# Cached memory in seven buffers with its heads side by side, and a convolution spread over more stages, in a one-core decoder trunk

## The reference

```python
def conv_branch(glu, prev, dw_w, dw_b, ln_g, ln_b):
    xp = jnp.concatenate([prev, glu], axis=1)
    y = lax.conv_general_dilated(xp, dw_w[:, None, :], window_strides=(1,), padding='VALID',
                                 dimension_numbers=('NWC', 'WIO', 'NWC'),
                                 feature_group_count=CONV_WIDTH)
    y = layer_norm(y + dw_b, ln_g, ln_b)
    return jax.nn.silu(y), xp[:, -(CONV_K - 1):]

def cross_attention(xn, mem_k, mem_v, w_xq, w_xo):
    B, T, _ = xn.shape
    q = (xn @ w_xq).reshape(B, T, N_X_HEADS, X_HEAD_DIM)
    s = jnp.einsum('bqhd,bkhd->bhqk', q, mem_k).astype(jnp.float32) * X_SCALE
    p = jax.nn.softmax(s, axis=-1).astype(mem_v.dtype)
    o = jnp.einsum('bhqk,bkhd->bqhd', p, mem_v).reshape(B, T, D_MODEL)
    return o @ w_xo
```

## Time and profile before

| what | value |
|---|---|
| median of 3 runs (lowest to highest) | 2113.44 us (2112.59 to 2114.67) |
| the profiled execution: time, span | 2116.94 us, 2115.4 us |
| mean granted TensorE clock | 0.941 |
| busy: PE, PEld, DVE, ACT, POOL | 89%, 81%, 46%, 24%, 6% of the span |
| chain that ended last, by engine | PE 81%, DVE 8%, ACT 4%, issue 3%, DMA 3% |
| moved by DMA | 187.11 MB, mean 88 GB/s |

### The profile page before, as it was taken

One profiled execution on the slowest core, in us unless ns is written; L12 is line 12 of the kernel. 1 busy time (PEld: TensorE's weight loads), 2 busy tenths in 40 slices (PEclk: granted clock), 3 DMA queues, 4 the chain that ended last, 5 costly groups with the idle time before them and its releaser, 6 DMA issues.

```text
span 2115.4 us, 33154 instructions
## 1 busy us (share of the span) xinstructions
PE 1872.2 (89%) x13009; PEld 1705.1 (81%) x13009; DVE 969.3 (46%) x1131; ACT 500.1 (24%) x762; POOL 137.0 (6%) x200
## 2 busy tenths in 40 slices
PE   6699997887777897899896996999999999999993
PEld 5699895666554796799763995999999999999992
DVE  2625677887445528532320329343223343233445
ACT  3421114665334211310431224111000100001122
POOL 0000002211121002000001002000000000000001
PEclk7899998999899898899997998999999999999995
DMA  6311116655484312401125022121111111111004
GB/s 159 123 40 60 59 60 190 213 169 161 151 284 164 122 40 66 153 20 63 36 76 203 20 55 87 40 59 40 40 52 47 40 42 58 40 40 55 30 15 164
DMA packets 133052, 187.11 MB, mean 88 GB/s; under 512 B 7912, under 2 KB 99242, under 8 KB 132454
## 3 DMA queue, kind: packets, MB, share of 16 engines
q1 hardware_dynamic: 112816, 103.96, 15.8%
q0 software_dynamic: 19312, 81.31, 11.4%
q10 hardware_dynamic: 846, 0.73, 0.1%
HBM read 165.65 MB, written 20.74 MB: 88 GB/s over the span
## 4 chain that ended last, share of the span: by engine, by line
PE 81%; DVE 8%; ACT 4%; issue 3%; DMA 3%; SPq 0%; POOL 0%; DVEq 0%; ACTq 0%; POOLq 0%
PE PS L1480 19%; PE PS L1481 19%; PE PS L1482 19%; PE PS L1470 7%; PE PS L1557 2%; PE PS L1636 2%; DMA bias_rows<-BVEC 2%; PE PS L1666 2%; PE PS L1870 1%; PE PS L1616 1%; PE PS L1846 1%; PE PS L1740 1%; PE PS L1830 1%; PE PS L1495 1%; PE PS L1497 1%
## 5 line engine op out<-in xcount | busy, mean ns | idle before, releaser
L1480 PE MATMUL PS<-XH,WH 128*128 128x352 f32 x1992 | 643.1, 323 | 0.0
L1481 PE MATMUL PS<-XL,WH 128*128 128x352 f32 x1992 | 638.5, 321 | 0.0
L1482 PE MATMUL PS<-XH,WL 128*128 128x352 f32 x1992 | 638.2, 320 | 0.0
L1000 DVE CAST WH<-RAW 128x1024 fp32r<-128x1024 f32 x128 | 97.2, 760 | 737.2 <-PE PS L1482 711.3
L1481 PEld LDWEIGHTS PS<-XL,WH 128*128 128x128 f32 x1992 | 374.3, 188 | 0.0
L1480 PEld LDWEIGHTS PS<-XH,WH 128*128 128x128 f32 x1992 | 373.7, 188 | 0.0
L1482 PEld LDWEIGHTS PS<-XH,WL 128*128 128x128 f32 x1992 | 373.4, 187 | 0.0
L1002 DVE TENSOR_TENSOR WL<-RAW,WH 128x1024 fp32r<-128x1024 f32 x128 | 158.9, 1242 | 4.4
L1115 DVE SCALAR_TENSOR_TENSOR CY<-GP,DW,CY 128x1024 f32<-128x1024 f32 x124 | 158.4, 1278 | 0.5 <-DVE CY L1118 0.5
L1480 PE MATMUL PS<-HH,WH 128*128 128x352 f32 x462 | 149.0, 323 | 0.0
L1481 PE MATMUL PS<-HL,WH 128*128 128x352 f32 x462 | 148.1, 321 | 0.0
(11 more groups left out here) (299 smaller groups left out, 2403.8 us busy)
## 6 DMA issues: line engine op xcount, KB each, us to landing
PG<-in_cache_k SPq DMA_DIRECT2D x64, 256.0 KB, 3.0
PG<-in_cache_k POOLq DMA_DIRECT2D x64, 256.0 KB, 3.9
PG<-in_cache_v SPq DMA_DIRECT2D x64, 256.0 KB, 4.6
PG<-in_cache_v POOLq DMA_DIRECT2D x64, 256.0 KB, 4.9
RAW<-in_w_gate SPq DMA_DIRECT2D x22, 512.0 KB, 4.0
RAW<-in_w_up SPq DMA_DIRECT2D x22, 512.0 KB, 5.2
RAW<-in_w_in SPq DMA_DIRECT2D x20, 512.0 KB, 4.8
h_spill<-H POOLq DMA_DIRECT2D x2, 4224.0 KB, 12.9
```

What stands on the lines that cost most here:

```text
L1000: dve.tensor_copy(WH[v % 2][:, :, :], raw).then_inc(hi_done, 1)
L1480: pe.matmul(out, WH[u][:, k, :], xh[:, k, cols], start=(k == 0), stop=False)
L1481: pe.matmul(out, WH[u][:, k, :], xl[:, k, cols], start=False, stop=False)
L1482: mm = pe.matmul(out, WL[u][:, k, :], xh[:, k, cols], start=False, stop=(k == kt - 1))
```

## The change

**Cross-attention.** CKV has seven buffers, and SyncE's queue loads them: keys 0 and 1 before the pairs of w_xo, the other keys behind three of the four pairs, then the values as buffers come free, and the fourth pair last. The cached keys come first on TensorE, ahead of the prompt's blocks: 16 turns per batch in a row, copies shared by ScalarE (heads 0 and 1) and VectorE (heads 2 and 3) into eight CKT buffers, then eight matmuls with the four heads in neighbouring groups of 32 rows. The prompt's scores read Y itself, XSCALE is multiplied in when the queries are scaled, and the maximum comes out negated. The scores of block q + 2 stand between the turns and the values of block q. The cached values stand ahead of block 7's turns.

**Convolution.** The samples' part becomes 12 wide instructions in the input projection. The prompt's taps are 18 in the input projection (ahead of the splits), 8 in stretch 1 (two of four channels per slot), one in the gap, four in stretch 2 (one channel per slot). Sums over the channels and the subtraction of the mean stand behind stretch 2.

```diff
-        CKV = [at(f"CKV{i}", [P, 2, D], F32, R1 + 8192 * i) for i in range(2)]
-        Q2S = [at(f"Q2S{i}", [P, KT, P], F32, R1 + 16384 + 4096 * i) for i in range(2)]
...
+        CKV_AT = [R2B + 16384, R2B + 24576] + [R1 + 8192 * i for i in range(4)] + [RC + 2336]
+        CKV = [at(f"CKV{i}", [P, 2, D], F32, off) for i, off in enumerate(CKV_AT)]
...
+        CKT = [at(f"CKT{i}", [P, 2, NMEM], F32, R1 + 32768 + 2048 * i) for i in range(2 * NH)]
...
+        def key_buffer(b):
+            return b % (DB - 1)
+
+        def value_buffer(b):
+            return (b + 1) % (DB - 1)
...
-            stream(io["w_xo"][0], "xo")
...
+            def memory_in(src, b, n):
+                sp.dma_start(CKV[n][:, :, :], src[b]).then_inc(buf_in[2 * n], 16)
+
+            sp.wait_ge(n_x["y_scaled"], KT)
+            sp.wait_ge(n_x["summed"], KT)
+            for b in range(2):
+                memory_in(ck, b, b)
+            w_xo = io["w_xo"][0]
+            for s in range(3):
+                pair_in(PAIR0["xo"] + s, s % 2, columns(w_xo, s % 2, 256 * s))
+            sp.wait_ge(tile_done, TILE0["xo"] + AHEAD)
+            for b in range(2, DB - 2):
+                memory_in(ck, b, b)
+            sp.wait_ge(psum_free, TILE0["xo"] + AHEAD)
+            memory_in(ck, DB - 2, DB - 2)
+            sp.wait_ge(ck_turned, NH)
+            memory_in(ck, DB - 1, 0)
+            for b in range(DB - 1):
+                n = value_buffer(b)
+                sp.wait_ge(ck_turned, NH * (b + 2))
+                memory_in(cv, b, n)
+            sp.wait_ge(cv_used, 1)
+            memory_in(cv, DB - 1, value_buffer(DB - 1))
+            pair_in(PAIR0["xo"] + 3, 1, columns(w_xo, 1, 256 * 3))
             first = 0
...
-            for b in range(2, DB):
-                pool.wait_ge(ck_turned, 4 * (b - 1))
-                pool.dma_start(CKV[b % 2][:, :, :], ck[b]).then_inc(ck_in[b % 2], 16)
...
-                pool.dma_start(CKV[b % 2][:, :, :], cv[b]).then_inc(ck_in[b % 2], 16)
+            pool.wait_ge(cs_done, DB)
+            pool.memset(PTZ[:, :, :, :], 0.0).then_inc(yz_ok, 1)
...
+            def conv_tap(j, c):
+
+                dve.wait_ge(conv_step, CT * j + c + 1 - CT + AHEAD_C)
+                dve.scalar_tensor_tensor(out=CY[:, c, 0:TP], in0=GP[:, c, ds(j, TP)], scalar=DW[:, ds(CT * j + c, 1)],
+                                         in1=CY[:, c, 0:TP], op0=ALU.mult, op1=ALU.add).then_inc(conv_step, 1)
...
+            def conv_samples():
+
+                def products(c):
+                    return QK[:, NH + c, 0:TS * CK].rearrange("p (b t j) -> p b t j", b=DB, t=DS)
+
+                def sums(c):
+                    return QK[:, NH + c, TS * CK:TS * CK + TS]
+
+                for c in range(CT):
+                    g = GS[:, c, :, :]
+                    windows = bass.AP(tensor=g.tensor, offset=g.offset,
+                                      ap=[g.ap[0], [CK - 1 + DS, DB], [1, DS], [1, CK]])
+                    w = DW[:, c:CK * CT:CT].unsqueeze(1).unsqueeze(1).to_broadcast([P, DB, DS, CK])
+                    dve.tensor_tensor(products(c), windows, w, ALU.mult).then_inc(conv_new, 1)
+                for c in range(CT):
+                    dve.wait_ge(conv_new, c + 1)
+                    dve.tensor_reduce(sums(c).rearrange("p (b t) -> p b t", b=DB), products(c), AX.X, ALU.add)\
+                        .then_inc(conv_new, 1)
+                for c in range(CT):
+                    dve.wait_ge(conv_new, CT + c + 1)
+                    dve.tensor_tensor(CY[:, c, TP:T], CY[:, c, TP:T], sums(c), ALU.add).then_inc(conv_new, 1)
 
             dve.wait_ge(cy_ok, CT)
             dve.wait_ge(glu_done, 2 * CT)
+            dve.wait_ge(h_spilled, 16)
+            dve.sem_inc(conv_step, AHEAD_C)
+            conv_samples()
             with dve.Fori(0, 3) as i:
                 for v in range(4):
+                    conv(6 * i + v + v // 2)
+                    if v % 2:
+                        conv(6 * i + v + v // 2 + 1)
                     split_at(8, i, v + 2)
-                    if v == 0:
-                        conv(5 * i)
-                    conv(5 * i + v + 1)
...
-                    conv(tap)
+                for j, c in taps:
+                    conv_tap(j, c)
                 if qb < QT - 1:
                     att_out(h, qb + 1)
                 dve.wait_ge(p_done, 2 * s + 2)
@@ -1185,7 +1214,8 @@
                 stage_batches(i)
                 for qb in reversed(range(QT)):
                     e = QT - 1 - qb
...
-                                         in1=tok3(CY[:, c, :]), op0=ALU.mult, op1=ALU.add).then_inc(mg_v, 1)
+            conv(26)
             dve.wait_ge(sm_a, SM_EXP)
             dve.tensor_tensor(DSUM, DSUM, DSUMN, ALU.add).then_inc(sm_v, 1)
             dve.wait_ge(sm_v, 9)
@@ -1237,7 +1263,7 @@
                                     .rearrange("p g (k c) -> p (g k) c", c=P)
...
                         .then_inc(v_staged, 1)
-                    att_slot(h, qb)
+                    att_slot(h, qb, ((27 + 2 * (h - 2) + e // 4, e % 4),))
                 dve.wait_ge(v_used, PAGES * 4 * (h - 1))
                 dve.tensor_copy(OB[:, :], PS[:, 7, :]).then_inc(ob_ok, 1)
...
+
+            dve.wait_ge(mg_p, 1)
+            dve.wait_ge(conv_step, CT * CK + AHEAD_C)
+            for c in range(CT):
+                dve.scalar_tensor_tensor(out=tok3(CY[:, c, :]), in0=bc3(0), scalar=-1.0 / 512,
+                                         in1=tok3(CY[:, c, :]), op0=ALU.mult, op1=ALU.add).then_inc(mg_v, 1)
...
-                dve.tensor_reduce(XMX[s], sc, AX.X, ALU.max).then_inc(xq_v, 1)
-                dve.wait_ge(xq_v, 2 * q + 1)
-                dve.tensor_scalar(XNM[s], XMX[s], -XSCALE, None, ALU.mult).then_inc(x_negmax, 1)
+                dve.tensor_reduce(XNM[s], sc, AX.X, ALU.max, negate=True).then_inc(x_negmax, 1)
...
             pe.wait_ge(p_done, 2 * 2 * QT)
-            pe.wait_ge(conv_step, 8 * CK)
-            for c in range(CT):
-                x = sum_over_channels(0, CY[:, c, :], c == 0, c == CT - 1)
-            x.then_inc(mg_p, 1)
             for c in range(8):
...
+            pe.wait_ge(p_done, 2 * NH * QT)
+            pe.wait_ge(conv_step, CT * CK + AHEAD_C)
+            for c in range(CT):
+                x = sum_over_channels(0, CY[:, c, :], c == 0, c == CT - 1)
+            x.then_inc(mg_p, 1)
             pe.wait_ge(ob_out, 2)
             for h in range(NH):
...
+            def memory_turn(b):
+
+                n = key_buffer(b)
+                pe.wait_ge(buf_in[2 * n], PAGES_IN + (32 if b == DB - 1 else 16))
+                for h in range(NH):
+                    if b:
+                        pe.wait_ge(ck_taken_a if h < 2 else ck_taken_v, 2 * (b - 1) + h % 2 + 1)
+                    for d in range(2):
+                        for a in range(2):
+                            c = 2 * h + d
+                            x = turn(PS[:, 2 + h, NMEM * d + P * a:NMEM * d + P * a + P], CKV[n][:, a, P * c:P * c + P])
+                    x.then_inc(ck_turned, 1)
+
+            def memory_scores(b):
+
+                pe.wait_ge(ck_taken_a, 2 * b + 2)
+                pe.wait_ge(ck_taken_v, 2 * b + 2)
+                for d in range(2):
+                    for h in range(NH):
+                        x = pe.matmul(PS[32 * h:32 * h + 32, 6, 0:NMEM], YZ[:, 2 * h + d, TS * b:TS * b + TS],
+                                      CKT[NH * (b % 2) + h][:, d, :], start=(b == 0 and d == 0),
+                                      stop=(b == DB - 1 and d == 1))
+                x.then_inc(cs_done, 1)
+
+            def memory_values(b):
+
+                n = value_buffer(b)
+                pe.wait_ge(buf_in[2 * n], PAGES_IN + (48 if n == 0 or b == DB - 1 else 32))
+                for a in range(2):
+                    for h in range(NH):
+                        x = pe.matmul(PS[32 * h:32 * h + 32, 0, 0:NMEM], PTZ[:, a, h, TS * b:TS * b + TS],
+                                      CKV[n][:, a, NMEM * h:NMEM * h + NMEM],
+                                      start=(b == 0 and a == 0), stop=(b == DB - 1 and a == 1))
+                x.then_inc(cv_used, 1)
...
+            memory_turn(0)
+            memory_turn(1)
+            pe.wait_ge(yz_ok, 2)
             for b in range(DB):
...
+                memory_scores(b)
+                if b + 2 < DB:
+                    memory_turn(b + 2)
+            cross_scores(0)
+            cross_scores(1)
+            pe.wait_ge(xsm_v, XSM_SCALED)
             for a in range(2):
-                x = turn(PS[:, 1, P * a:P * a + P], XS[:, P * a:P * a + P])
+                x = turn(PS[:, 7, P * a:P * a + P], XS[:, P * a:P * a + P])
             x.then_inc(xsm_p, 1)
-            pe.wait_ge(xsm_v, 6)
-            for b in range(DB):
-                pe.wait_ge(ck_in[b % 2], 64 + 16 * (b // 2) + 16)
-                for h in range(NH):
+            for q in range(QT):
+                if q == QT - 1:
```

(49 more changed lines are left out.)

170 lines of the change are left out of this document (50 added, 120 removed).

## The result

The changed kernel takes 2058.20 us (median of 4 runs, 2057.13 to 2060.13), the kernel before 2113.49: a ratio of 0.9736, 95% interval 0.9722 to 0.975. Forecast were 2060 and a range from 2046 to 2076. The profiled execution took 2058.20, its span is 2056.3, the mean granted clock 0.950. The profiled execution of before had taken 2116.94, 3.5 above its median, so the two traces lie 58.7 apart and the medians 55.3.

The account below looks back on a forecast made before the run. The prediction took TensorE's queue plus its waits as the bound. From the profiled 2116.94, -57 (cross stage) and +3 (convolution) gave 2063, or 2060 against the median; likeliest case 2050 to 2070, range 2046 to 2076.

Parts of the forecast that it names:

- Start of the keys: Cross stage: TensorE can begin the cached keys when the last query scaling ends, at 1002.5.
- A batch of keys: Cross stage: 16 turns (2.2 us) and 8 matmuls side by side (0.98), 3.2 us per batch, 25.4 for eight.
- The 3.42 us of serial work: Cached keys: estimated serial time of eight matmuls done in 0.98; the skill's factors would add about 5 or 11 us.
- Loads: Cached keys: key 7 lands at 1024 to 1025, TensorE needs it at 1026, so loads are narrowly hidden.
- The rival with a load every 5.5 us: Cached keys: SyncE's queue is the limit, each load waiting for the one before; +14, 2074; chance 11%.
- Blocks: Cross stage, prompt blocks: the 1.11 us copy lies under the scores, so the period falls from 9.28 to 8.17 us.
- The rival that VectorE and ScalarE set the round: Prompt blocks: the period stays 9.28 because ScalarE and VectorE carry the round; 2067; chance 10%.
- Values and end: Cross stage's end: cached values 7.8 us, block 7 6.3, tail and hand-overs 4.0; output projection starts at 1112, -57.
- Convolution: Input projection to stretch 2's end: gap -4.0 with 0.4 given back, mean behind stretch 2 +6.7; together +3 (0.5 to 6).
- the term for input projection and stretch 1: Convolution: input projection costed at 0 (up to 26 without cover), stretch 1 at 0, bounded by a gain of 10.
- The third rival, that stretch 1 profits: Stretch 1: VectorE's emptier queue releases ScalarE and then TensorE sooner; up to -10, 2050; chance 8%.
- The low clock: Cross stage: rival that TensorE's clock stays at 1.2 GHz, doubling about 98 us of work; 2158; chance 3%.

Follow-up runs that it names:

- two buffers: The changed kernel with cached keys and values going through the two early buffers instead of seven, each loaded again when its batch is used: 2079.29 us, ratio 0.983.
- the old order: The changed kernel with the scores of prompt block q + 1 ahead of block q's turns, nothing between turns and values: 2065.32 us, ratio 0.976.
- the cross-attention alone: The kernel before with only the cross-attention part of the change: 2059.82 us, ratio 0.9733.
- the convolution alone: The kernel before with only the convolution part (taps spread, wide sample instructions, mean behind stretch 2): 2115.93 us, ratio 1.0007.

## Why the prediction was right, step by step

- **Start of the keys**: 1002.5 forecast, 1004.34 measured. The one step that failed in kind: the diff moved GpSimd's memset next to VectorE's cast, and I had priced GpSimd's list at nothing. The cast took 1.9 us longer for it.
- **A batch of keys**: 3.2 forecast, 2.90 measured; the turns in a row take 1.90, not 2.2. The conversion of the earlier trace rows to full clock was right, 1.00 against 0.98. The 3.42 us of serial work in the prediction are a slip: four pairs of 0.98 are 3.92, which is four times the 0.98 of all eight side by side, and its 5 and 11 us follow from 3.92. Eight matmuls in one group take 3.57, so four groups gain 3.57 times. The Trainium skill ("TensorE: Matmul & The Clock Gate", "Measured speedup vs the span model") has 3.07 for four row tiles and 2.38 for three column tiles, and this case's figure lies above both. The cold start cost 32 turns 6.4 us instead of 3.8. The keys ended at 1031.2, with 1031 forecast, and that is luck: a start 1.8 late and 0.9 of waiting for loads stood against batches that were 2.2 quicker in all and a cold start of 2.6 where 3.0 was charged.
- **Loads**: 0.9 us of waiting, none forecast. The queue moved 412 GB/s, more than the 372 that I had taken, and still key 2 and key 4 came a little late: the slow cast held up the loads as well, for the third pair of w_xo was issued at 1003.10, behind VectorE's WL, and not at 1001.53 as before. The rival with a load every 5.5 us fell; with two buffers, where the loads come nearest to it, the keys end 3 us later and not 14.
- **Blocks**: 8.17 forecast, 7.90 measured. The wait went as forecast, and in the chain the values, which no longer start behind a wait, take 3.57 instead of 3.84. (The scores that begin at 1021.47 are block 2's, not block 1's as the prediction says; the period is the same.) The rival that VectorE and ScalarE set the round fell with the old order, which gave 9.28 back.
- **Values and end**: 8.4 us from 1093.09 to 1101.5, 7.8 with at most 0.7 more forecast. First matmul of xo at 1112 forecast, 1111.38 measured.
- **Convolution**: the gap -3.6 forecast (-4.0, of which 0.4 was given back for a low clock), -4.1 measured; the sample weights' matmuls behind it took 9.48 against 9.25, 0.2 more. The end +6.7 forecast, +6.8 measured (11.9 from the end of OB's turns to the variance's end before, 18.7 after). Mis-sized was the term for input projection and stretch 1, costed at 0 with a gain of 10 as its bound: stretch 1 ends 3.2 us sooner (513.19 to 509.96). Of the 3.2, 2.2 are there when stretch 1's first scores start (335.56 to 333.34), and 0.6 of these only because the profiled execution after began its input projection sooner (68.17 against 68.76). So the term is -1.6 at the hand-over and -1.0 in the stretch. With +0.5 from the sample weights to OB's turns, costed at 0 but for the 0.4 above, the convolution comes to about +0.5 and not +3. GpSimd's timeline says where about one of the 1.6 was: the copy CNEW, beside VectorE's last taps before,

```profile
325.93 1.26 POOL L565 COPY CNEW<-GS 128x128 f32<-128x128 f32 x1
...
327.33 0.37 PE L1470 MATMUL PS<-IDENT,GP 128*30 128x128 f32 x1 [4.00 <-POOL CNEW L565]
```

and with VectorE idle after:

```profile
325.50 0.30 POOL L595 COPY CNEW<-GS 128x128 f32<-128x128 f32 x1
...
325.95 0.27 PE L1502 MATMUL PS<-IDENT,GP 128*30 128x128 f32 x1 [3.04 <-POOL CNEW L595]
```

TensorE's wait for that copy is 0.96 us shorter, as the copy is. The eight turns of GP and CNEW behind it take 1.0 us instead of 1.9, at a granted clock of 1.00 instead of 0.50. In the cross-attention alone, with the taps of before, the copy takes 1.26 and the wait 4.00 again; in the convolution alone they are 0.30 and 3.04. That the taps beside it make the copy slow is argued from these rows; no run changed only that. The third rival, that stretch 1 profits, was therefore right in sign, at 1.0 us of its 10 in the stretch proper.
- **The low clock**: 0.57 for 7 us, then 1.00 throughout the keys and the blocks. The rival did not come about; with two buffers it did, in the values alone.
- **What is luck in 2060**: by the traces the forecast was 2063, and 2058.20 came. Of the 5 us, about 2.6 are the convolution's mis-sized term. Another 2.0 lie ahead of the input projection (0.6) and behind the cross stage (1.4), where nothing was changed: two executions differ by that much. Against the medians the miss shows as 2 us only, since the profiled execution of before was one of the slower ones.

## What to carry to other kernels

Where several small matmuls use a part of the array each, put them next to each other with nothing wide between: their order among themselves is free, their column groups are not. A wait for a copy was covered here by the scores of two blocks ahead, which need nothing of it. And work on the path, like the mean, is best put where its engine already waits: the subtraction of the mean cost 7 us with its sums behind stretch 2, and in VectorE's idle 9 the gap kept its length. When instructions of one engine go away, look at what moves up beside which other: the list of an engine that is 6% busy cost 1.9 us here by an overlap that had not been there.

## What had not been expected of the hardware

- Eight narrow matmuls (32 columns of weights each) over four column groups take 1.00 us with the groups alternating and 1.02 with two of each group in a row; in one group 3.57.
- A VectorE cast of 128x1024 took 2.59 us beside a GpSimd memset of 2.01, and 0.69 alone; a 128x128 GpSimd copy 1.26 beside VectorE's three-operand taps, and 0.30 alone.
- With several 1 MB loads in SyncE's queue the core drew 412 GB/s over 21 us; with the two on GpSimd's queue and one pair of weights it had been 372.
